# A second transformer block in one kernel: local attention with split values as weights and transposed results

## The reference, cut to what matters

```python
scores = scores + alibi[None, None]                       # local heads
scores = jnp.where(valid[None, :, None, None], scores, -jnp.inf)
m = jnp.maximum(jnp.max(scores, axis=-1, keepdims=True), sink)
p = jnp.exp(scores - m)
denom = jnp.sum(p, axis=-1, keepdims=True) + jnp.exp(sink - m)
p = (p / denom).astype(v.dtype)
out = jnp.einsum('bnkgqs,bnskd->bnqkgd', p, vb)
...
mixed = jnp.concatenate([out_a.reshape(b, s, A_Q_W), out_b.reshape(b, s, B_W)], axis=-1)
x = x + jnp.einsum('bse,ed->bsd', mixed, w_out)
```

## Time and profile before

| | us |
|---|---|
| median of 3 runs | 2722.82 (2721.86 to 2727.66) |
| the profiled execution's own time | 2724.15 |
| its span, first to last instruction | 2722.3 |
| TensorE busy | 2633.6 (97%) |
| VectorE busy | 1837.4 (67%) |
| ScalarE busy | 1326.2 (49%) |
| mean granted clock of TensorE | 0.991 |

### The profile page before, as it was taken

One profiled execution on the slowest core, in us unless ns is written; L12 is line 12 of the kernel. 1 busy time (PEld: TensorE's weight loads), 2 busy tenths in 40 slices (PEclk: granted clock), 3 DMA queues, 4 the chain that ended last, 5 costly groups with the idle time before them and its releaser, 6 DMA issues. The chain is left out here.

```text
span 2722.3 us, 37072 instructions
## 1 busy us (share of the span) xinstructions
PE 2633.6 (97%) x13612; PEld 2193.7 (81%) x13612; DVE 1837.4 (67%) x2469; ACT 1326.2 (49%) x1952; POOL 405.3 (15%) x359
## 2 busy tenths in 40 slices
PE   8999999999999899999999999899999999999999
PEld 7888876877788888888888788778888788888887
DVE  5761365457524888888888857566625875857878
ACT  3111243567432577877787422555533553525353
POOL 0222212100230122222221022300020000000000
PEclk9999999999999999999999999999999999999999
DMA  3115124311452699999999332100032616253451
GB/s 128 54 47 182 40 74 131 127 39 52 137 179 109 237 378 380 386 381 371 374 371 348 139 105 68 39 1 1 1 132 66 266 49 248 71 187 135 157 183 62
DMA packets 142456, 437.83 MB, mean 161 GB/s; under 512 B 23408, under 2 KB 45680, under 8 KB 110576
## 3 DMA queue, kind: packets, MB, share of 16 engines
q1 hardware_dynamic: 125312, 402.40, 41.0%
q0 software_dynamic: 10656, 20.99, 2.2%
q10 hardware_dynamic: 6352, 12.58, 1.2%
HBM read 387.68 MB, written 66.06 MB: 167 GB/s over the span
## 5 line engine op out<-in xcount | busy, mean ns | idle before, releaser
L2729 DVE TENSOR_TENSOR w_lo<-w_raw,w_hi 128x2048 fp32r<-128x2048 f32 x192 | 437.2, 2293 | 60.3 <-ACT w_hi L2663 59.3
L2663 ACT ACTIVATE w_hi<-w_raw 128x2048 fp32r<-128x2048 f32 x187 | 355.8, 1925 | 39.5 <-PE banks L2790 39.5
L3660 PE MATMUL banks<-b_parts,a_parts 128*128 128x512 f32 x1344 | 306.9, 390 | 6.3 <-DVE a_parts L3715 6.3
L3660 PE MATMUL banks<-a_parts,b_parts 128*128 128x512 f32 x1344 | 306.0, 389 | 2.3 <-DVE a_parts L3715 1.2
L3660 PEld LDWEIGHTS banks<-b_parts,a_parts 128*128 128x128 f32 x1344 | 251.8, 188 | 60.9 <-DVE a_parts L3715 8.8
L3660 PEld LDWEIGHTS banks<-a_parts,b_parts 128*128 128x128 f32 x1344 | 252.0, 188 | 55.2 <-DVE a_parts L3715 1.6
L3689 ACT ACTIVATE b_parts<-w_quarter 128x1024 fp32r<-128x1024 f32 x112 | 118.6, 1059 | 281.4 <-PE banks L3660 266.8
L766 POOL TENSOR_TENSOR w_lo<-w_raw,w_hi 128x512 fp32r<-128x512 f32 (+2 forms) x132 | 158.6, 1207 | 576.6 <-ACT w_hi L745 575.4
L745 ACT ACTIVATE w_hi<-w_raw 128x512 fp32r<-128x512 f32 (+2 forms) x132 | 73.9, 573 | 324.0 <-PE banks L824 306.0
L3709 DVE TENSOR_TENSOR b_parts<-w_quarter,b_parts 128x1024 fp32r<-128x1024 f32 x112 | 136.9, 1222 | 132.5 <-ACT b_parts L3689 132.5
L824 PE MATMUL banks<-w_hi,act_hi 128*128 128x512 f32 (+1 forms) x576 | 219.9, 382 | 6.0 <-POOL w_lo L766 3.7
(11 more groups left out here) (545 smaller groups left out, 5560.8 us busy)
## 6 DMA issues: line engine op xcount, KB each, us to landing
w_raw<-in_w SPq DMA_DIRECT2D x192, 1024.0 KB, 7.4
a_parts<-scratch_x_parts SPq DMA_DIRECT2D x42, 1024.0 KB, 4.8
w_raw<-in_w_in SPq DMA_DIRECT2D x80, 256.0 KB, 2.7
w_quarter<-in_w_up SPq DMA_DIRECT2D x16, 1024.0 KB, 6.9
w_quarter<-in_w_down SPq DMA_DIRECT2D x16, 1024.0 KB, 8.0
scratch_x_parts<-a_parts SPq DMA_DIRECT2D x14, 1024.0 KB, 5.1
scratch_gateT<-gate_staged SPq DMA_DIRECT2D x32, 256.0 KB, 2.2
gate<-scratch_gateT SPq DMA_DIRECT2D x32, 256.0 KB, 3.6
```

The lines of the kernel that those rows point to most:

```text
L2663: act.activation(hi[c % SLOTS][:, :], raw[c % TILES][:, :], ACT.Copy).then_inc(hi_done, 1)
L2729: dve.tensor_tensor(lo[c % SLOTS][:, :], raw[c % TILES][:, :], hi[c % SLOTS][:, :].bitcast(F32), ALU.subtract).then_inc(lo_done, 1)
L3660: mm = pe.matmul(out, left, right, start=(start and n == 0), stop=(stop and n == 2))
```

## The change

The values of the local heads are split into high and low parts in place, and for each key head stand as one 128-column operand: 64 columns high, 64 low. They become the stationary operand, and the transposed probabilities of four heads (512 columns) the moving one, once their high part (made by ScalarE) and once their low part (by VectorE). The result is transposed: rows 0 to 63 are the products with the high values, rows 64 to 127 those with the low ones. ScalarE copies one half across (`cross`), VectorE adds the other (`out`). Since rows of the result are no longer queries, the division moves ahead of the transposes (`normalise`). The results are stored as the output projection needs them, which leaves 32 transposes there; `MixedRows` makes their parts one row at a time, ScalarE and POOL take weight tiles in between, and the first tile's rows wait each for their own parts. In the last block the window units come after 3 and 6 of the 8 forgetting units. The old `turn_rows` is deleted (not shown). A window unit's output on VectorE is taken one turn later than before, ahead of `turn_out`.

```diff
 
@@ -768,6 +768,8 @@
 
             if head:
                 head.gpsimd(pool)
+            if pool_before:
+                pool_before(pool)
             for i, (tile, units, n) in enumerate(turns):
                 if i >= started:
                     low(pool, i)
@@ -811,6 +813,8 @@
                     b = tile.b0 + u - units[0]
                     if tile.first and freed[b]:
                         pe.wait_ge(free, freed[b])
+                    for s, count in tile.rows_ready.get(u, ()):
+                        pe.wait_ge(s, count)
                     if tile.kind == "nat":
                         t = slice(u * P, (u + 1) * P)
                         out = v.bank[b][:, :tile.cols]
...
@@ -3248,8 +3189,7 @@
         self.g, self.i, self.window = g, i, True
         self.keys = min(2, i + 1) * P
         self.width, self.exps = self.keys * (AH // AKV), AH // AKV + 1
-        first = max(0, i - 1)
-        self.blocks = [(a * self.keys + (j - first) * P, j, a, j == first, j == i) for a in range(AH // AKV) for j in range(first, i + 1)]
+        self.key_tiles = list(range(max(0, i - 1), i + 1))
 
 
 def attention2_stage(v):
-    v.out_a, v.out_b = v.qa, v.qb[:, :, :, :].rearrange("p t h c -> p t (h c)")
+    a_lo, a_hi = at("a_lo", FREE + 61.5, [P, 2, N], F32R), at("a_hi", RINGS + 12, [P, 2, S], F32R)
+    values = at("values", FREE + 16, [P, NT, KVF_W], F32R)
+    v.out_aT, v.out_b = v.qa, v.qb[:, :, :, :].rearrange("p t h c -> p t (h c)")
@@ -3281,9 +3223,11 @@
             units += [window[0], forget[0], window[1], forget[1]]
         elif n == 4:
             units += [forget[0], window[0], forget[1], window[1]]
-        else:
+        elif i < NT - 1:
             half = len(forget) // 2
             units += forget[:half] + window[:1] + forget[half:] + window[1:]
+        else:
+            units += forget[:3] + window[:1] + forget[3:6] + window[1:] + forget[6:]
         windows_at.append(starts[i] + units[starts[i]:].index(window[0]))
         forget_at.append(starts[i] + units[starts[i]:].index(forget[0]))
     n_units = len(units)
...
+    splits_values = {0: 0, **{windows_at[t] - 1: t for t in range(1, NT)}}
+
+    def is_window(p):
+        return 0 <= p < n_units and units[p].window
...
+    def aT_hi(p, b):
+        return a_hi[:, p % 2, b * N:(b + 1) * N]
+    def by_side(x, r, side):
+        return x[r, :].rearrange("p (m e q) -> p m e q", m=2, e=2)[:, :, side, :]
+    def own_heads(u, r):
+        c = 2 * u.g * P
+        return v.out_aT[r, u.i, c:c + 2 * P].rearrange("p (m q) -> p m q", m=2)
...
+                if units[p].window:
+                    for b in range(len(units[p].key_tiles)):
+                        if b:
+                            act.wait_ge(turned_high, high_upto[p + 1])
+                        act.activation(aT_hi(p, b), (LOW, HIGH)[b], ACT.Copy).then_inc(hi_turned, 1)
+                    return
                 c = min(units[p].width, N)
+            def cross(p):
+                u = units[p]
+                act.wait_ge(weighed, p + 1)
+                for side in range(2):
+                    act.activation(own_heads(u, SIDES[side]), by_side(v.bank[6 + p % 2], SIDES[1 - side], side), ACT.Copy).then_inc(crossed, 1)
 
                 if u.window:
+                    act.activation(snk[:, s, :], snk[:, s, :], ACT.Exp).then_inc(exped, 1)
                     for a in range(HALF):
                         c = slice(a * u.keys, (a + 1) * u.keys)
                         act.activation(q[:, c], q[:, c], ACT.Exp, bias=nmax[:, s, a:a + 1], accum_out=sums[:, s, a:a + 1]).then_inc(exped, 1)
-                    act.activation(snk[:, s, :], snk[:, s, :], ACT.Exp).then_inc(exped, 1)
                 else:
                     if p >= 3:
+                if is_window(p - 3):
+                    cross(p - 3)
+            turn_out(n_units - 2)
+            cross(n_units - 3)
+            turn_out(n_units - 1)
 
...
             def turn_out(p):
+                if units[p].window:
+                    if p >= 2:
+                        dve.wait_ge(weighed, p - 1)
+                    for b in range(len(units[p].key_tiles)):
+                        dve.wait_ge(hi_turned, hi_upto[p] + b + 1)
+                        dve.tensor_tensor(a_lo[:, b, :], (LOW, HIGH)[b], aT_hi(p, b).bitcast(F32), ALU.subtract).then_inc((low_read, high_read)[b], 1)
+                    return
...
                 if u.window:
-                    then(dve.tensor_tensor(inv[:, s, :], sums[:, s, :], snk[:, s, :], ALU.add))
-                    then(dve.reciprocal(inv[:, s, :], inv[:, s, :]))
-                    c = u.g * HALF * HD
-                    dve.tensor_tensor(v.out_a[:, u.i, c:c + HALF * HD].rearrange("p (a d) -> p a d", d=HD),
-                                      v.bank[6 + p % 2].rearrange("p (a g d) -> p a g d", g=AKV, d=HD)[:, :, u.g, :],
-                                      inv[:, s, :].unsqueeze(2).broadcast_to([P, HALF, HD]), ALU.mult).then_inc(weigh_read, 1)
+                    dve.wait_ge(crossed, 2 * windows_upto[p + 1])
+                    for side in range(2):
+                        made = own_heads(u, SIDES[side])
+                        (dve.tensor_tensor(made, by_side(v.bank[6 + p % 2], SIDES[side], side), made, ALU.add)
+                         .then_inc(*((weigh_read, 1) if side else (link_a, 1))))
                 else:
+
+            def normalise(p):
+                u, s, q = units[p], p % 4, probs[:, p % 3, :]
+                for a in (0, 2):
+                    dve.wait_ge(exped, exped_upto[p] + 1 + a + 2)
+                    own, c = slice(a, a + 2), slice(a * u.keys, (a + 2) * u.keys)
+                    then(dve.tensor_tensor(inv[:, s, own], sums[:, s, own], snk[:, s, own], ALU.add))
+                    then(dve.reciprocal(inv[:, s, own], inv[:, s, own]))
+                    x = q[:, c].rearrange("p (a k) -> p a k", a=2)
+                    dve.tensor_tensor(x, x, inv[:, s, own].unsqueeze(2).broadcast_to([P, 2, u.keys]), ALU.mult).then_inc(normed, 1)
+
+            def split_values(t):
+                dve.wait_ge(ops.tr_ready, ops.turned_before(t, 2) + 2)
+                for g in range(AKV):
+                    src = v.kvf[:, t, (AKV + g) * HD:(AKV + g + 1) * HD]
+                    hi, lo = (values[:, t, g * P + c:g * P + c + HD] for c in (0, HD))
+                    then(dve.tensor_copy(hi, src))
+                    ins = dve.tensor_tensor(lo, src, hi.bitcast(F32), ALU.subtract)
+                    ins.then_inc(values_split, 1) if g else then(ins)
+                if is_window(p - 1):
+                    normalise(p - 1)
+                if is_window(p - 4):
+                    out(p - 4)
                 if p >= 2:
                     turn_out(p - 2)
                 if prepares(p):
                     ops.dve_part(dve, *prepares(p), (LOW, HIGH))
-                if p >= 3:
+                if p >= 3 and not is_window(p - 3):
                     out(p - 3)
+                if p in splits_values:
+                    split_values(splits_values[p])
+                if u.window:
+                    pe.wait_ge(normed, 2 * windows_upto[p + 1])
+                    free_banks(p - 1)
+                    for b in range(len(u.key_tiles)):
+                        for a in range(HALF):
+                            c = a * u.keys + b * P
+                            mm = pe.transpose((LOW, HIGH)[b][:, a * P:(a + 1) * P], probs[:, p % 3, c:c + P], v.ident[:, :])
+                        mm.then_inc((turned_low, turned_high)[b], 1)
+                    return
+                if u.window:
+                    pe.wait_ge(values_split, u.i + 1)
+                    for b, j in enumerate(u.key_tiles):
+                        vals = values[:, j, u.g * P:(u.g + 1) * P]
+                        pe.matmul(v.bank[6 + p % 2][:, :], vals, aT_hi(p, b), start=(b == 0), stop=False)
+                        mm = pe.matmul(v.bank[6 + p % 2][:, :], vals, a_lo[:, b, :], start=False, stop=(j == u.i))
+                    mm.then_inc(weighed, 1)
+                    return
                 for c, j, a, first, last in u.blocks:
-                    if u.window:
-                        vals, w = v.kvf[:, j, AKV * HD:2 * AKV * HD], P
-                    else:
-                        vals, w = v.vb[:, j, (u.h + a) * HD:(u.h + a + 1) * HD], HD
+                    vals, w = v.vb[:, j, (u.h + a) * HD:(u.h + a + 1) * HD], HD
...
+class MixedRows:
+
+    BY_POOL = (3, 6)
+    ACT_ORDER = ("b0", "a0", "b1", "a1", "w0", "b2", "a2", "b3", "a3", "b4", "a4", "w1", "b5", "a5", "b6", "a6", "b7", "a7", "w2", "w3")
+    POOL_ORDER = ("w0", "a3", "w1", "a6", "w2", "w3")
+
+    def __init__(self, v, ring):
+        sem = v.sem
+        self.v, self.ring = v, ring
+        self.turned, self.b_hi, self.b_lo = sem("b_rows_turned"), sem("b_rows_hi"), sem("b_rows_lo")
+        self.a_hi, self.a_lo, self.a_lo_pool = sem("a_rows_hi"), sem("a_rows_lo"), sem("a_rows_lo_pool")
```

(73 more changed lines are left out.)

60 lines of the change are left out of this document (7 added, 53 removed).

## The result

The changed kernel takes 2751.72 us (median, 2747.31 to 2754.51) against 2722.78 us for the kernel before in the same comparison: a ratio of 1.0101, 95% interval 1.0085 to 1.0117, so about 29 us slower. The forecast was 2733.5 us in a range up to 2748. The direction was right, the size was not.

A forecast was written before the change was run, and what follows sets the result against it. The prediction took TensorE, busy for 97% of the span, as the bound. Attention stage +16.5 us and output projection -5.5 us made +11 us on the median of 2722.82 us: 2733.5 us, range 2712 to 2748.

The forecast's parts named there:

- The work: Attention stage: weighing local values in fewer, longer matmuls saves 11.6 us on TensorE's path.
- The waits: Attention stage: TensorE's new waits for VectorE and ScalarE, +26.9 us in all.
- case A: Middle of a block: TensorE waits on VectorE's division and high-bank copy, 0.4 to 0.75 us; block 7, 0.45 twice.
- Case B: Preparations following local units (21, 31, 41): start 2.3 us later until banks are read; 7.1 us including unit 19.
- Case C: Preparations 23, 33 and 43: the output moved ahead puts 0.8 us before the high copy; 2.4 us.
- Unit 50: Last block's preparation: unit 49's division stands ahead of the copy it waits for; 2.0 us.
- Blocks 0 to 3: Early attention blocks: division, output and crossing copy delay TensorE's transposes and preparations, together 12.2 us.
- The clock: Attention stage: more and longer waits bring more stretches at 1.2 GHz; +1.5 us, from nothing to +10.
- the clock falls more often: Rival, attention stage: some six new waits each bring 3 us at 1.2 GHz; +9 us, 2742 us, chance 0.15.
- The waits being covered: Rival, attention stage: VectorE's chain fits under TensorE's work, so the matmul saving shows; 2710 us, chance 0.15.
- half as long: Rival, attention stage: added delay partly falls into old idle time, halving the waits; 2721 us, chance 0.2.
- The projection: Output projection: half the transposes and the barrier go, so its tiles start earlier; -5.5 us, bounds -7.4 and -3.

The follow-up runs named there:

- e3_fill: Changed kernel plus 46 unused identity products on TensorE in its longest waits, at nine preparations; 2738.2 us, ratio 1.0046 to the kernel before.
- e2_order: Changed kernel with VectorE's low parts or copy of HIGH put ahead of the division and the local output; 2727.93 us.
- e9_late: Changed kernel, reordered on VectorE, preparation steps shifted, one add and reciprocal, some filler matmuls; then ScalarE's crossing copy and VectorE's output moved later; 2730.08 us.

## Why the prediction was right and wrong

**The work** held: forecast -11.6, measured 224.7 - 213.1 = 11.6. That they agree to the tenth is chance: four weighing records take 1.0 us from start to start (1905.59 to 1906.60 in the changed kernel), not 0.93, which by the forecast's own sum makes 10.4, and the measured term is up to 1 us high, by the half clock that was counted while TensorE stood idle. The 25.9 us that the group shows for its 60 records are durations with their passage and no price.

**The waits** held in place and nearly in size: 26.9 forecast, 22.5 measured. The division took 1.99 us (2.0). In case A the waits of blocks 4 to 6 were 0.94, 0.69 and 0.50 us (0.4 to 0.75), those of block 7 0.39 each (0.45). Case B was 1.7 to 1.8 us each, 0.7 to 0.8 at the local unit's transposes and 1.05 at the preparation, where 0.25 stood before, not 2.3 more; that is over half of what the forecast has too much. Case C was 1.5 us in all (2.4). Unit 50 had 0.73 + 1.62 = 2.35, 0.25 before (2.0 more forecast). Blocks 0 to 3 wait 11.9 us more than before (12.2), and preparation 14, where a single wait of 0.47 us stood, has two, 2.5 us more (2.65):

```profile
1825.76 0.64 PE L2929 MATMUL banks<-ident,qb_aug 128*84 128x128 f32 x4 [0.47 <-ACT probsT L3291]
1828.92 1.08 PE L2929 MATMUL banks<-ident,qb_aug 128*84 128x128 f32 x4 [2.52 <-DVE probsT L3350]
```

**The clock is the step that failed.** It said "I take +1.5, from nothing to +10"; measured were 25.6 - 3.4 = 22.2 us. Two errors lie in it. The term set against the new loss that "much falls into waits anyway", and the rows show otherwise: the half clock falls on the work behind a wait, so that TensorE is busy for 48.9 of the 51.2 us. And the rival "the clock falls more often", with +9 on the forecast and a chance of 0.15, named the mechanism and the number of places, but had each as 3 us at 1.2 GHz. The clock fell at six places, at 1753.1, 1763.4, 1777.0, 1787.2, 1821.4 and 1978.4 us, and stayed down for 6.8 us at each but the fifth, where it was 17.1 us with a break of 3.4. The longest stretch, and the long one after it at full clock:

```profile
1828.20:1841.86 13.66, 12.94 (x50) 11.23 (x51) 6.26 (x15) 3.13 (x7) 0.73 (x2) 0.50 0.00 1
1841.86:1978.39 136.53, 119.16 (x865) 104.53 (x863) 104.11 (x299) 85.47 (x214) 8.31 (x14) 1.00 0.00 1
```

With 22.2 in place of 1.5 and 22.5 in place of 26.9 the stage's sum is the 33.1 that was measured; the 0.3 for the stage's end shows only in the gap behind it. The terms that the forecast names for its high end don't reach the 2748 us that it gives: 2742 and the 2.5 us from -5.5 to -3 in the projection make 2745. The waits being covered (0.15) and half as long (0.2) did not happen.

**The projection** was forecast at -5.5 and gave -6.5. The 2 us that I set aside for subtractions beside POOL were too many: the six of them average 769 ns against 684 for the eight that read a bank, 0.5 us in all, and the longest took 0.98 us, so none stood for a whole operation of POOL (1.3 us). From the group lines:

```profile
L3584 DVE TENSOR_TENSOR act_lo<-banks,act_hi 128x512 fp32r<-128x512 f32 x8 | 5.4, 684 | 3.6 <-ACT act_hi L3559 3.4
...
L3568 DVE TENSOR_TENSOR act_lo<-qa,act_hi 128x512 fp32r<-128x512 f32 x6 | 4.6, 769 | 0.0
```

With the measured terms the change is -11.6 + 22.5 + 22.2 - 0.3 - 6.5 = +26.3 us in its two stages. The other 2.6 us of the medians' difference no run attributes. So the direction came out right and the waits nearly so; the size failed by the clock.

## What to carry to other kernels

When a change queues work on a helper engine ahead of an answer that TensorE waits for, price the waits twice: for themselves, and for the half clock on the work behind them, which here cost as much again. Before taking work out of such a chain, try its order: moving one copy ahead of the division gave back 24 of 29 us. Where a long wait can't be removed, matmuls of no use in it may pay, as in e3_fill.

## What the runs showed of the hardware

Waits of 1.1 to 2.6 us between busy stretches were enough to bring TensorE from 2.4 to 1.2 GHz: in the changed kernel each of the six places at half clock begins inside a wait of this length or at most 0.9 us behind it (after the 2.38 us before 1763.65 the clock stood at 0.50), and e3_fill took away 22.2 us of loss with 8.8 us of idle time. The Trainium skill (TensorE: Matmul & The Clock Gate, "A second HAM failure mode: psum-queue depth-cycling") tells of a kernel whose frequent short idles between groups of matmuls made the clock go back and forth; by that rule, the trace agrees in part. The clock did go back and forth, with no wait longer than 2.6 us. But in this kernel 24 waits of 0.25 to 1.05 us from 1841.86 us on, 15.6 us in all, left it at 1.0, and it fell only at 1978.39, behind one of 1.62 us. Nor does the length of a wait settle it: in e2_order one of 1.05 us is followed by 6.8 us at half clock, while in e3_fill waits of 1.92 and 1.62 us (before 1818.23 and 1960.81) are followed by none. And the sum of idle time says little: e9_late with 29.8 us lost 11.9 to the clock, e3_fill with 30.1 lost 3.4. What around a wait decides it, no run shows.
